# Experts with more than 64 tokens: weight blocks held in the array, 96 tokens' high and low parts streamed side by side

## What is computed

```python
def swiglu(h, w1, w3, w2):
    return (jax.nn.silu(h @ w1) * (h @ w3)) @ w2

def moe_ffn(h, router, w1, w3, w2):
    t = h.reshape(B * S, D)
    logits = (t @ router).astype(jnp.float32)
    top_v, top_i = lax.top_k(logits, TOP_K)
    top_w = jax.nn.softmax(top_v, axis=-1)
    gates = jnp.sum(jax.nn.one_hot(top_i, N_EXPERTS) * top_w[..., None], axis=1)
    for e in range(N_EXPERTS):
        out = out + gates[:, e:e + 1] * swiglu(t, w1[e], w3[e], w2[e])
```

## Time and profile before

| | |
|---|---|
| median of 2 runs | 1559.4 us (1559.08 to 1559.72) |
| the profiled execution | 1559.46 us |
| its span, first to last instruction | 1557.7 us |
| mean granted clock of TensorE, share of full | 0.992 |
| experts, first matmul to the last step | 652.8 to 1554 us of the span |

### The profile page before, as it was taken

One profiled execution on the slowest core, in us unless ns is written; L12 is line 12 of the kernel. 1 busy time (PEld: TensorE's weight loads), 2 busy tenths in 40 slices (PEclk: granted clock), 3 DMA queues, 4 the chain that ended last, 5 costly groups with the idle time before them and its releaser, 6 DMA issues.

```text
span 1557.7 us, 22471 instructions
## 1 busy us (share of the span) xinstructions
PE 1516.2 (97%) x8524; PEld 1269.9 (82%) x8524; DVE 1261.7 (81%) x1411; ACT 1082.6 (70%) x1302; POOL 16.4 (1%) x34
## 2 busy tenths in 40 slices
PE   7999999999899999699999999999999999999998
PEld 7999959999899996588777788777888777888675
DVE  4888745545577864698899998999988999988997
ACT  5775443333458651487899977889877889877896
POOL 4000000000000000000000000000000000000000
PEclk9999999999999999799999999999999999999999
DMA  9544345555444541499999999999999999999993
GB/s 262 193 156 179 136 145 207 188 189 190 142 180 145 184 162 68 191 421 421 381 414 415 421 421 349 371 395 414 422 415 348 376 389 418 420 399 350 375 408 161
DMA packets 64870, 460.45 MB, mean 296 GB/s; under 512 B 7434, under 2 KB 7670, under 8 KB 9462
## 3 DMA queue, kind: packets, MB, share of 16 engines
q1 hardware_dynamic: 63878, 457.22, 74.5%
q0 software_dynamic: 832, 1.74, 0.8%
q10 hardware_dynamic: 48, 0.02, 0.0%
HBM read 457.89 MB, written 1.05 MB: 295 GB/s over the span
## 4 chain that ended last, share of the span: by engine, by line
PE 80%; DVE 13%; ACT 4%; DMA 1%; issue 1%; POOL 0%; SPq 0%; DVEq 0%; ACTq 0%
PE bank L1063 10%; PE bank L1064 10%; PE bank L1067 10%; PE bank L773 8%; PE bank L775 8%; PE bank L774 8%; DVE w_lo L610 7%; PE bank L1016 7%; PE bank L1019 6%; PE bank L825 4%; PE bank L1095 2%; PE bank L1103 2%; PE bank L1028 2%; ACT w_hi L541 1%; DVE w_lo L549 1%
## 5 line engine op out<-in xcount | busy, mean ns | idle before, releaser
L610 DVE TENSOR_TENSOR w_lo<-arena,w_hi 128x1024 fp32r<-128x1024 f32 x527 | 618.9, 1217 | 43.8 <-ACT w_hi L604 37.6
L604 ACT ACTIVATE w_hi<-arena 128x1024 fp32r<-128x1024 f32 x527 | 535.1, 1054 | 84.1 <-PE bank L1067 67.3
L549 DVE TENSOR_TENSOR w_lo<-ring,w_hi 128x2048 fp32r<-128x2048 f32 x88 | 201.4, 2290 | 144.6 <-ACT w_hi L541 143.5
L773 PE MATMUL bank<-h_hi,w_hi 128*128 128x256 f32 x992 | 283.3, 286 | 3.6 <-DVE w_lo L549 1.8
L774 PE MATMUL bank<-h_lo,w_hi 128*128 128x256 f32 x992 | 280.6, 283 | 0.0
L775 PE MATMUL bank<-h_hi,w_lo 128*128 128x256 f32 x992 | 280.6, 283 | 0.0
L541 ACT ACTIVATE w_hi<-ring 128x2048 fp32r<-128x2048 f32 x88 | 168.2, 1914 | 114.3 <-PE bank L775 80.2
L773 PEld LDWEIGHTS bank<-h_hi,w_hi 128*128 128x128 f32 x992 | 190.2, 192 | 6.0 <-issue 2.9
L774 PEld LDWEIGHTS bank<-h_lo,w_hi 128*128 128x128 f32 x992 | 190.3, 192 | 0.5
L775 PEld LDWEIGHTS bank<-h_hi,w_lo 128*128 128x128 f32 x992 | 190.2, 192 | 0.0
L1063 PE MATMUL bank<-w_hi,h_hi 128*128 128x512 f32 x448 | 177.6, 396 | 2.6 <-ACT w_hi L604 2.6
(11 more groups left out here) (297 smaller groups left out, 2179.0 us busy)
## 6 DMA issues: line engine op xcount, KB each, us to landing
arena<-in_moe_w SPq DMA_DIRECT2D x270, 1024.0 KB, 8.6
ring<-in_moe_w SPq DMA_DIRECT2D x66, 1024.0 KB, 8.9
ring<-in_ffn_w SPq DMA_DIRECT2D x33, 1024.0 KB, 4.8
ring<-in_w_gate SPq DMA_DIRECT2D x32, 1024.0 KB, 4.8
ring<-in_w_in SPq DMA_DIRECT2D x15, 1024.0 KB, 4.9
ring<-in_w_branch SPq DMA_DIRECT2D x8, 1024.0 KB, 4.8
ring<-in_w_out SPq DMA_DIRECT2D x8, 1024.0 KB, 4.8
x_tok<-in_x SPq DMA_DIRECT2D x2, 512.0 KB, 3.7
```

Of the source, the lines that this page charges most:

```text
L549: nc.vector.tensor_tensor(w_lo[:, m % LO, :], raw, w_hi[:, m % HI, :].bitcast(F32), ALU.subtract)\
L604: nc.scalar.activation(half_hi[:, r % AHEAD, :], raw_of(n)[:, HALF * (m % 2):HALF * (m % 2) + HALF], ACT.Copy)\
L610: eng.tensor_tensor(half_lo[:, r % AHEAD, :], raw_of(m // 2)[:, HALF * (m % 2):HALF * (m % 2) + HALF], half_hi[:, r % AHEAD, :].bitcast(F3 ...
L773: pe.matmul(out_, a[0], b[0], start=start, stop=False)
```

## The change

For big experts, whose slots fall from 128 to 96 (`BIG`), h1 and h3 are computed the other way round. Blocks of 128x128 weights are held and tokens streamed: the 96 high parts and the 96 low parts lie side by side in `h_big_both`, so one matmul of 192 columns against a block of high weights gives high x high and, beside it, high x low; a matmul of 96 columns against the block of low weights is added to the first. A product fills two banks (`inner0` for h1, `inner1` for h3), each with two blocks of 96 high and 96 low columns, and there is one such pair for each product instead of two alternating banks.

The low columns are brought to the high ones by ScalarE's copy (`copy_low`) and a product with an identity (`join_big`). The results have the hidden units on the partitions already, so the transposes of big steps go; Silu, product and split work on 4 x 96 columns, the split from SBUF. The product with w2 holds 96 columns and streams 512 as before. The join of h1 stands behind the first half of h3, the join of h3 behind the first half of w2 (in step 0 right behind h3). TensorE waits for `prod_done` before h3 and, where a big step is concerned, for the Silu of the step before ahead of h1. The guards become 96 tokens for the largest count and 64 still for the fourth smallest.

```diff
+            def half_big(m, q, b):
+
+                r = ex.rank[m]
+                pe.wait_ge(half_hi_done, r + 1)
+                w, wl = half_hi[:, r % AHEAD, :], half_lo[:, r % AHEAD, :]
+                for k in range(2):
+                    for c in range(4):
+                        dst = big_at(b, c)
+                        pe.matmul(dst, w[:, MU * k + P * c:MU * k + P * c + P], h_big_both[:, 2 * q + k, :],
+                                  start=q == 0 and k == 0 and c % 2 == 0, stop=False, skip_group_check=True)
+                wait_half_lo(pe, m)
+                for k in range(2):
+                    for c in range(4):
+                        last = pe.matmul(big_at(b, c, BIG), wl[:, MU * k + P * c:MU * k + P * c + P], h_big_both[:, 2 * q + k, 0:BIG],
+                                         start=False, stop=q == 3 and k == 1, skip_group_check=True)
+                last.then_inc(half_used, 1)
...
+            def join_big(kind, i):
+
+                n = 2 * big_steps(i) + (kind == "h3") + 1
+                pe.wait_ge(lo_copied, n)
+                for a in range(2):
+                    high = inner_banks[int(kind == "h3")][:, a, 0:4 * BIG].rearrange("p (c x n) -> p c x n", c=2, x=2)[:, :, 0, :]
+                    low = act_lo[:, i % 2, 2 * BIG * a:2 * BIG * a + 2 * BIG].rearrange("p (c n) -> p c n", c=2)
+                    last = pe.matmul(high, eye_r[:, :], low, start=False, stop=True, skip_group_check=True)
+                last.then_inc(lo_joined, 1)
...
-                    if i // S_MOE in SMALL:
-                        last = pe.matmul(bank[2][:, P * c:P * c + FEW], hidden, fold[:, :], start=True, stop=True)
-                    else:
-                        last = pe.transpose(bank[2][:, P * c:P * c + P], hidden, ident)
+                    last = pe.matmul(bank[2][:, P * c:P * c + FEW], hidden, fold[:, :], start=True, stop=True)
...
-                            inner("h1", i, [(tile, 4 + i % 2)], ex.rank.get, e if s == 0 else None)
+                            inner_big("h1", i, e if s == 0 else None)
                     if 1 <= i < STEPS:
-                        turn_hidden(i - 1)
+                        if is_few(i - 1):
+                            turn_hidden(i - 1)
+                        pe.wait_ge(prod_done, i)
...
-                            inner("h3", i, [(tile, 6 + i % 2)], ex.rank.get)
+                            inner_big("h3", i)
...
-            with pe.If(most_tokens > CAP):
+            with pe.If(most_tokens > BIG):
...
+            def copy_low(kind, i):
+
+                fn(by_banks(act_lo[:, i % 2, 0:4 * BIG]), in_banks(kind, 1), ACT.Copy).then_inc(lo_copied, 1)
```

More of the change, by code:

```diff
@@ L199, in __init__, with ahead @@
         self.rank = {m: r for r, m in enumerate(self.split)}
+    def ahead(self, r):
+        return self.split[r] - (self.split[r - 1] if r else -1)
     def used(self, kind, i):
@@ L220, in sem @@
             return ctx.enter_context(nc.semaphore(name))
-        bank = [ctx.enter_context(nc.psum_tensor(f"bank{b}", [P, 512], F32)) for b in range(8)]
+        bank = [ctx.enter_context(nc.psum_tensor(f"bank{b}", [P, 512], F32)) for b in range(4)]
+        inner_banks = [ctx.enter_context(nc.psum_tensor(f"inner{b}", [P, 2, 512], F32)) for b in range(2)]
+        bank += [inner_banks[b // 2][:, b % 2, :] for b in range(4)]
         ring = sb("ring", [P, SLOTS, 2048])
@@ new lines, in inner_big @@
+            def inner_big(kind, i, gathers=None):
+                for q in range(4):
+                    if gathers is not None and q == 2:
+                        pe.wait_ge(hg_ready, 2 * gathers + 2)
+                    m, b = ex.first[(kind, i, 0)] + q, 4 if kind == "h1" else 6
+                    half_big(m, q, b)
+                    if kind == "h3" and q == 0:
+                        join_big("h1", i)
+            def join_big(kind, i):
[6 more added lines that the diff above has]
+                last.then_inc(lo_joined, 1)
@@ new lines, in outer_big @@
+            def outer_big(i, behind_first=None):
+                first, final = i % S_MOE == 0, i % S_MOE == S_MOE - 1
+                for c in range(4):
+                    block = slice(BIG * c, BIG * c + BIG)
+                    outs = [(act_hi[:, i % 2, block], act_lo[:, i % 2, block], slice(512 * n, 512 * n + 512), bank[n][0:BIG, :])
+                            for n in range(2)]
+                    m = ex.first[("w2", i, 0)] + c
+                    half(m, ex.rank[m], outs, lambda x: first and c == 0, lambda x: final and c == 3)
+                    if c == 0 and behind_first:
+                        behind_first()
@@ L1077, in inner, with outer @@
                     m = ex.first[(kind, i, 0)] + q
-                    half(m, rank(m), outs, lambda x: q == 0 and x % 2 == 0, lambda x: q == 3 and x % 2 == 1)
-            def outer(i, acts, rank):
+                    half(m, m, outs, lambda x: q == 0 and x % 2 == 0, lambda x: q == 3 and x % 2 == 1)
+            def outer(i, acts):
                 first, final = i % S_MOE == 0, i % S_MOE == S_MOE - 1
@@ L1085, in outer @@
                     m = ex.first[("w2", i, 0)] + c
-                    half(m, rank(m), outs, lambda x: first and c == 0, lambda x: final and c == 3)
+                    half(m, m, outs, lambda x: first and c == 0, lambda x: final and c == 3)
             def gather(e, c, b):
@@ L1102, in spread @@
                 for e in experts:
-                    last = pe.matmul(bank[b][:, :], gatesT[e % 2][:, t, :], y_slot[e % 2][:, 512 * n:512 * n + 512],
+                    slots = slice(0, slots_of(e))
+                    last = pe.matmul(bank[b][:, :], gatesT[e % 2][slots, t, :], y_slot[e % 2][slots, 512 * n:512 * n + 512],
                                      start=(e == experts[0]), stop=(e == experts[-1]))
@@ L1213, in all_tokens @@
                     if i < STEPS:
-                        inner("h1", i, [(tiles[t], 4 + t) for t in range(TT)], int)
-                        inner("h3", i, [(tiles[t], 6 + t) for t in range(TT)], int)
+                        inner("h1", i, [(tiles[t], 4 + t) for t in range(TT)])
+                        inner("h3", i, [(tiles[t], 6 + t) for t in range(TT)])
                     if i >= 1:
@@ L2019, in next_lo @@
                     r = ex.rank[u] + AHEAD
-                    split_half_lo(dve, ex.split[r], r, ex.split[r] - ex.split[r - 1])
+                    split_half_lo(dve, ex.split[r], r, ex.ahead(r))
             def next_lo_all(u):
@@ L2052, in lower @@
                 else:
-                    tt(act_lo[:, i % 2, :], bank[2][:, :], act_hi[:, i % 2, :].bitcast(F32), ALU.subtract).then_inc(act_done, 1)
+                    block = slice(0, 4 * BIG)
+                    tt(act_lo[:, i % 2, block], sil[:, i % 2, block], act_hi[:, i % 2, block].bitcast(F32), ALU.subtract)\
+                        .then_inc(act_done, 1)
             def gathered_experts():
                 gathered_lo(0, 0, 5)
-                for m in range(2):
-                    split_half_lo(dve, m, m)
+                for r in range(2):
+                    split_half_lo(dve, ex.split[r], r, ex.ahead(r))
                 gathered_lo(0, 1, 7)
-                for m in range(2, AHEAD):
-                    split_half_lo(dve, m, m)
+                for r in range(2, AHEAD):
+                    split_half_lo(dve, ex.split[r], r, ex.ahead(r))
                 weights()
@@ L2076, in gathered_experts @@
                         tt(sil[:, i % 2, :], bank[6 + i % 2][:, :], sil[:, i % 2, :], ALU.mult).then_inc(prod_done, 1)
+                    big = i + 1 if done == ("w2", 0, 1) else 0 if i == 0 and done == ("h3", 1, 1) else STEPS
+                    if big < STEPS and not is_few(big):
+                        dve.wait_ge(lo_joined, 2 * big_steps(big) + 2)
+                        dve.wait_ge(sil_done, big + 1)
+                        hidden = by_banks(sil[:, big % 2, 0:4 * BIG])
+                        tt(hidden, in_banks("h3", 0), hidden, ALU.mult).then_inc(prod_done, 1)
                     if done == ("w2", 0, 1) and s in (1, 2) and e in SMALL:
```

120 lines of the change are left out of this document (79 added, 41 removed).

## The result

The changed kernel takes 1683.6 us (1681.65 and 1685.58) against 1559.4: ratio 1.080, 95% interval 1.078 to 1.082. It is slower by 124 us; the forecast was 90 slower (1649, range 1636 to 1692). The profiled execution took 1681.65 us.

The account below looks back on a forecast made before the run. TensorE was taken to bound big experts, splits and loads small ones. 28 big steps x (3.18 + 0) + 0.85 once made 90 us; 1559.5 + 90 = 1649.5, stated as 1649 us, range 1636 to 1692.

Parts of the forecast that it names:

- The load sets the pitch: Inner products of big experts: 16 matmuls a half at 0.110 us, 1.76 instead of 1.362; +3.18 us a step.
- The step: A big expert's step without gather goes from 16.8 to 20.0 us, a big expert from 119 to 141.
- The outer product: Product with w2 in big steps: still six matmuls of 512 columns a half, narrower held operand; 0 us.
- Joins, copies, new waits: Big steps: joins add 0.44 us, dropped transposes save 0.44; copies hidden, except a wait at step 0, +0.85 once.
- The clock: Rival: in big steps the clock falls, mostly 1.2 GHz, a half at 3.2 us; +412 us, 1970; 5%.
- the rival of 1686: Rival: in big experts' inner products and joins a fixed part adds to the load, pitch 0.120 us; +126 us; 16%.
- Small experts: Small experts start as now, hang on splits and loads, and stay at 105 us; 0 us.
- Loads hidden under streams: Rival: in big steps float32r loads run under the stream before, a half costs 1.17 us; 1531 us; 4%.
- the single pass lost under 256 columns: Rival: narrow float32r matmuls of the inner products lose their single pass, a half costs 4.05 us; +602, 2160 us; 6%.
- the path through all experts: Rival: an expert exceeds the guard of 96 tokens, so all tokens run through all experts; about 2490 us; 3%.

Follow-up runs that it names:

- e5: The changed kernel with the product with w2 holding 128 columns instead of 96 in big steps; 1683.9 us.
- e1: The changed kernel with the blocks of low weights streaming 192 columns instead of 96, as many loads; 1658.1 us.
- e3: The changed kernel without the matmuls against the low weights in h3 of big steps; 1575.8 us, one run.
- e2: The changed kernel with each 192-column matmul cut into two of 96, 24 loads a half instead of 16; 2343.9 us, one run.
- e4: The changed kernel with 36 unread matmuls of 512 columns in TensorE's idle times before the experts; 1687.4 us.
- e7: The changed kernel with 24 unread matmuls of 512 columns behind the second half of the first step; 1665.2 us.
- run 96: Not a separate run: the words are from "e2's one run 96 alone", where 96 is the columns behind each load; e2 took 2343.9 us.
- e6: The kernel before the change, with 36 unread matmuls of 512 columns in TensorE's idle times ahead of the experts; 1561.2 us.

## Why the prediction was right, and what it missed

**What bounds it.** Right. The trace after is TensorE end to end in big experts, and the experiments moved the time with TensorE's loads and its clock; another held width moved nothing (e5).

**The load sets the pitch (the core of the sum).** Right, shown from both sides: more columns behind as many loads changed nothing (e1: 0.111), fewer loads saved 0.111 each where no join waited (e3), more loads cost 0.109 each at full clock (e2). The pitch taken was 0.110; it came out at 0.112 in most halves (1.79) and at 0.111 over the eight of a step. Over 28 x 128 loads that is 3 us. The upper bound of 0.120, a fixed part on top of the load, didn't come.

**The step.** Forecast 20.0 (16.34 / 3 + 14.08 + 0.44 = 19.97), measured 20.25 (changed steps without a gather). Of the 0.28 more, w2's halves with the join of h3 are 0.13 (5.80 instead of 5.67), the join of h1 0.05 (0.27 instead of 0.22), and the eight inner halves 0.10 (14.18 instead of 14.08). The outer product was put at 0, and with 96 columns held its halves came out 0.02 to 0.03 slower; why stays open (e5). A big expert was forecast at 141 and takes 144.6, on a cut that gives 120.0 for before where the forecast started from 119: 24.6 more, where 28 x 3.18 / 4 = 22.3 was forecast. For all four, 98 instead of 89.

**Joins, copies, new waits.** Right: of all joins only step 0's waited for the copy, 0.6 us, with 0.85 forecast for copy and start. ScalarE and VectorE stayed hidden.

**The clock: the step that failed.** The prediction had the clock as a rival of all big steps (1970, 5%) and, in the sum, as full throughout: "Against: the granted clock is 1.00 (2.4 GHz) through both kinds of expert". That row is of 512-column streams already at full clock; it says nothing on how the clock gets back after the idle time at the routing, where the trace had it at 0.55. So the sum priced the first two steps at full clock on a row that doesn't bear on them; the term it put at 0 measured 25 us. In the changed kernel sixteen halves of the first two steps ran at 3.42 us instead of 1.79: 16 x 1.63 = 26 us. e1, where the clock came back at once, is 25 below the changed kernel, and at 1658.1 lies within 1 us of 1559.4 + 98. So the overshoot of 34 us against the forecast is 25 of clock and 9 of longer steps. In the big steps after the first two the clock held at full in the trace, as forecast; in e2's one run, with 96 columns behind each load, it fell in step after step.

**Partly luck.** 1683.6 lies inside the range, and 2 us from the rival of 1686, for another reason than the forecast or that rival gave. The upper end was made for a pitch of 0.120 and waits at the joins; neither came, and the clock, which no term of the range covered, took that room. By the time alone the wrong rival would have seemed confirmed; the pitch in the trace rules it out.

**Small experts.** Right: 104.3 before and 104.2 after between the first matmuls of h1, with VectorE busy 99.8 and 99.3 of it.

**Other rivals.** Loads hidden under streams and the single pass lost under 256 columns are out by the pitches; the path through all experts is out, since the trace has the inner products of `gathered_experts` (L1090, L1095).

The Trainium skill, "TensorE: Matmul & The Clock Gate", section "Back-to-back issue gap", gives about 81 ns for a load and matmul of 128 columns. It doesn't hold for float32r here: 0.109 us at 96 columns (e2) and 0.111 at 192 (e1), each at full clock. The Trainium skill, "TensorE: Matmul & The Clock Gate", section "LDWEIGHTS (loading the stationary operand)", gives the columns held divided by 1.2 in ns, an estimate of 107 ns for 128. The traces at full clock agree within 5 ns.

## What to carry to other kernels

Count loads beside columns: with float32r and 128 columns held, no half of narrow matmuls took less than about 0.11 us for each of them. So price both ways of holding. A half of six wide matmuls took 1.36; with narrow ones against held weights, an estimate from these rows is that up to 12 loads (12 x 0.111 = 1.33) would have been no slower; 16 were, though they stream a quarter fewer columns. Where a kernel goes from idle time straight into matmuls that stream little behind each load, look at the granted clock there, for TensorE can be busy and stay at half speed; 24 wide matmuls whose result nobody reads were worth 18 us here, and where they stand matters: ahead of the gap they gained nothing (e4). And widening the streams from 96 to 192 columns under a load cost nothing here, and the clock came back.

## What the runs showed of the hardware

The clock depended on what streamed, not on whether TensorE was busy. After the idle gap it stayed at half for 61 us with TensorE busy 60.9 of 61.5: 56 us of the mixture of 192 and 96 columns, until the first wide matmuls of w2 had run for 5 us. It came back within 4 us where the same loads had 192 columns each (e1), inside the first h3 where only that product had 192 behind each load (e3), and during 24 matmuls of 512 (e7). From full clock the mixture of 192 and 96 held it for the rest of the experts in the traces kept, and in e2's one run 96 alone lost it in step after step. What exactly the chip weighs is left open.

At half clock the load's pitch was 0.213 and at full clock 0.109 (e2), nearly twice: the load slows down with this clock.

Wide matmuls in the idle times ahead of the experts brought a gap of 4.64 us (e4) and one of 3.35 (e6) in TensorE's stream, for which the trace shows no wait, in the middle of the first half of the first product, and none there where such matmuls stood behind two halves of it (e7). It may be the arrival of instructions, while the transfers run at 420 GB/s. The traces speak for it: a packet of 16 KB on the instruction queue q8 starts 2.3 us before TensorE goes on in both (653.99 and 656.27 in e4, 651.60 and 653.93 in e6), and 2.5 us before the first inner product of the changed kernel (646.05 and 648.56). No experiment tests it.
